# Norm chains of a two-block transformer kernel: row scaling and squares on opposite row halves, and scaled transposes that VectorE writes to SBUF

## What is computed

```
def rms_norm(x, g):
    y = xf * lax.rsqrt(jnp.mean(xf * xf, axis=-1, keepdims=True) + EPS)
    return y * g
...
for l in range(DEPTH_2):
    h = modulate(rms_norm(x, mix_pre_g[l]), sh1, sc1)        # h * (1 + scale) + shift, per column
    p = h @ w_in[l]
    ...
    x = x + g1 * rms_norm(y, mix_post_g[l])
    h2 = modulate(rms_norm(x, ffn_pre_g[l]), sh2, sc2)
    x = x + g2 * rms_norm(sq_relu_mlp(h2, w_ff1[l], w_ff2[l]), ffn_post_g[l])
    # and the same for a second stream, the context, in layer 0
```

## Time and profile before

| | |
|---|---|
| median of three runs | 2186.89 us (2186.88 to 2187.64) |
| the profiled execution's own time | 2187.78 us |
| its span in the profile | 2185.8 us |
| mean granted TensorE clock | 0.988 |
| TensorE, VectorE, ScalarE busy | 95%, 72%, 52% |

### The profile page before, as it was taken

How to read it: one execution, slowest core, us unless ns; L and a number is a source line. 1 busy time by engine, 2 the same in 40 slices (tenths; PEclk the granted TensorE clock), 3 DMA queues, 4 the chain that set the end, 5 groups by cost and what they waited for, 6 DMA issues and landing times.

```text
span 2185.8 us, 31557 instructions
## 1 busy us (share of the span) xinstructions
PE 2086.1 (95%) x12389; PEld 1785.9 (82%) x12389; DVE 1566.2 (72%) x2436; ACT 1129.9 (52%) x1571; POOL 97.2 (4%) x184
## 2 busy tenths in 40 slices
PE   7998989999999999999999999899999999997997
PEld 6776879888877788988887788698978878877996
DVE  5566466577679978655687898765677789976565
ACT  5554444445575446544557544454545674454543
POOL 3100001110000000000000000000000000000000
PEclk9999999999999999999999999999999999999999
DMA  7745467766666645677654444656555444454663
GB/s 253 225 148 188 146 223 249 235 190 203 216 211 193 195 151 168 222 220 227 189 179 130 145 135 142 214 157 191 170 174 184 131 143 126 154 164 145 189 187 106
DMA packets 206371, 394.36 MB, mean 180 GB/s; under 512 B 16471, under 2 KB 19219, under 8 KB 206224
## 3 DMA queue, kind: packets, MB, share of 16 engines
q1 hardware_dynamic: 198624, 381.74, 54.9%
q0 software_dynamic: 7600, 10.61, 1.7%
HBM read 390.98 MB, written 1.30 MB: 179 GB/s over the span
## 4 chain that ended last, share of the span: by engine, by line
PE 83%; DVE 8%; ACT 5%; issue 2%; DMA 2%; DVEq 0%; ACTq 0%; SPq 0%
PE gps L1142 15%; PE gps L1144 14%; PE gps L1143 14%; PE gps L1149 9%; PE gps L1150 9%; PE gps L1151 9%; PE aps L981 2%; PE aps L1104 2%; DVE wlo L1958 2%; PE aps L937 2%; DVE Yc L1801 2%; ACT whi L1464 1%; PE aps L1080 1%; PE aps L1111 1%; PE aps L1067 1%
## 5 line engine op out<-in xcount | busy, mean ns | idle before, releaser
L1958 DVE TENSOR_TENSOR wlo<-raw,whi 128x1024 fp32r<-128x1024 f32 (+1 forms) x648 | 763.3, 1186 | 449.6 <-ACT whi L1464 447.2
L1464 ACT ACTIVATE whi<-raw 128x1024 fp32r<-128x1024 f32 (+1 forms) x648 | 662.6, 1028 | 662.7 <-PE gps L1144 420.2
L1142 PE MATMUL gps<-whi,ohi 128*128 128x512 f32 x1624 | 656.2, 404 | 9.5 <-DVE olo L1829 5.0
L1144 PE MATMUL gps<-whi,olo 128*128 128x512 f32 x1624 | 634.8, 391 | 0.0
L1143 PE MATMUL gps<-wlo,ohi 128*128 128x512 f32 x1624 | 634.4, 391 | 0.0
L1149 PE MATMUL gps<-ohi,whi 128*128 128x256 f32 x1760 | 508.4, 289 | 1.0 <-issue 1.0
L1150 PE MATMUL gps<-olo,whi 128*128 128x256 f32 x1760 | 499.8, 284 | 0.0
L1151 PE MATMUL gps<-ohi,wlo 128*128 128x256 f32 x1760 | 499.5, 284 | 0.0
L1142 PEld LDWEIGHTS gps<-whi,ohi 128*128 128x128 f32 x1624 | 305.8, 188 | 87.2 <-issue 21.0
L1144 PEld LDWEIGHTS gps<-whi,olo 128*128 128x128 f32 x1624 | 305.5, 188 | 65.3
L1149 PEld LDWEIGHTS gps<-ohi,whi 128*128 128x128 f32 x1760 | 339.0, 193 | 20.0 <-issue 19.1
(11 more groups left out here) (284 smaller groups left out, 1544.9 us busy)
## 6 DMA issues: line engine op xcount, KB each, us to landing
raw<-w_in SPq DMA_DIRECT2D x232, 512.0 KB, 3.9
raw<-w_ff SPq DMA_DIRECT2D x192, 512.0 KB, 3.8
raw<-ada_w SPq DMA_DIRECT2D x96, 512.0 KB, 4.4
raw<-w_attn_o SPq DMA_DIRECT2D x24, 512.0 KB, 3.4
raw<-w_gmlp_o SPq DMA_DIRECT2D x24, 512.0 KB, 3.4
raw<-w_conv_o SPq DMA_DIRECT2D x24, 512.0 KB, 3.7
raw<-w_out SPq DMA_DIRECT2D x24, 512.0 KB, 4.7
raw<-w_gate SPq DMA_DIRECT2D x20, 512.0 KB, 4.1
```

The lines of the kernel that those rows point to most:

```text
L1142: mm(om, ah, whi[:, q, i, :], start=first, stop=False)
L1144: t = mm(om, al, whi[:, q, i, :], start=False, stop=last)
L1464: A_(part(whi, jb, q), raw_part(jb, q), ACT.Copy).then_inc(hi_done[q], 1)
L1958: tt(part(wlo, jb, q), raw_part(jb, q), f32(part(whi, jb, q)), ALU.subtract).then_inc(lo_done[q], 1)
```

## The change

1. `T` with a scale: VectorE alone reads the bank, tile by tile (k), applies scale and shift into a slot of 256 columns of `PTb` (four slots), ScalarE copies the slot to `ohi`, VectorE subtracts `ohi` from the slot into `olo`. VectorE's subtraction of tile k stands behind its scaling of tile k + 2. From the third bank on the scaling waits for the subtractions that free its slots.
2. `ycp`: VectorE takes row half 1 first, while ScalarE squares half 0; ScalarE squares half 1 behind it (`y_g`), VectorE takes half 0 behind the first square (`y_sq`).
3. `accy`: the addition is cut in row halves, and ScalarE's first square needs the first half only.
4. `po`: the job j = 0 multiplies and shifts its own sums of squares in advance, so that `po` needs one instruction (L1556) in place of L1552 and L1524.

```diff
@@ ScalarE @@
             def T(p):
-                if p.scale:
-                    wait(act, ("pp_cols", None, 0, 1) if p.scale[0] == "C1" else ("mf_c", None, 0, MODS[p.scale[1:3]] + 1))
                 for b in p.banks:
-                    wait(act, ev("t_pe", p, 4, b + 1))
                     if p.scale:
                         for i in range(2):
                             k = 2 * b + i
-                            t = A_(ohi[:, p.slot, k, :], aps[:, b, i * S:(i + 1) * S], ACT.Identity,
-                                   scale=column(p.scale, k), bias=column(p.shift, k) if p.shift else 0.0)
+                            act.wait_ge(sem["t_y"], 8 * p.of_kind + k + 1)
+                            A_(ohi[:, p.slot, k, :], scaled(k), ACT.Copy).then_inc(sem["t_h"], 1)
...
             def ycp(jb, g):
...
-                sum_squares(jb, tiles(g, 2))
+                sum_squares(jb, tiles(g, 2), lambda m: act.wait_ge(sem["y_g"], jb.n + 1) if m else None)
@@ VectorE @@
             def po(p):
...
-                link(tt(st[:, 5, 0:2], st[:, 5, 0:2], st[:, 5, 2:4], ALU.add))
-                w = rms(5, 2, 1.0 / D)
+                link(stt(st[:, 5, 0:2], st[:, 5, 2:4], CUBIC / D, st[:, 5, 0:2], ALU.mult, ALU.add))
+                w = st[:, 12, :]
+                rsqrt(w[:, 0:2], st[:, 5, 0:2], w[:, 8:10])
...
             def T(p):
...
+                    for b in range(5):
                         for i in range(2):
                             k = 2 * b + i
+                            if b < 4:
+                                if i == 0:
+                                    wait(dve, ev("t_pe", p, 4, b + 1))
+                                    if b > 1:
+                                        wait(dve, ev("t_lo", p, 4, b - 1))
+                                x = aps[:, b, i * S:(i + 1) * S]
+                                if p.shift:
+                                    t = ts(scaled(k), x, column(p.scale, k), column(p.shift, k), ALU.mult, ALU.add)
+                                else:
+                                    t = ts(scaled(k), x, column(p.scale, k), None, ALU.mult)
+                                t.then_inc(sem["t_y"], 1)
+                            if b:
+                                k -= 2
+                                dve.wait_ge(sem["t_h"], 8 * p.of_kind + k + 1)
+                                t = tt(olo[:, p.slot, k, :], scaled(k), f32(ohi[:, p.slot, k, :]), ALU.subtract)
+                                if i:
+                                    t.then_inc(sem["t_lo"], 1)
...
             def ycp(jb, g):
-                gain(jb, tiles(g, 2))
+                dve.wait_ge(used[NQ - 1], jb.i + 1)
+                gain(jb, tiles(g, 2), (1, 0))
...
-                tt(y, y, tiles(g, 2), ALU.add).then_inc(sem["y_add"], 1)
-                dve.wait_ge(sem["y_add"], jb.n + 1)
-                gain(jb, y)
+                for m in range(2):
+                    tt(y[:, m, :], y[:, m, :], tiles(g, 2)[:, m, :], ALU.add).then_inc(sem["y_add"], 1)
+                dve.wait_ge(sem["y_add"], 2 * jb.n + 2)
+                gain(jb, y, (0, 1))
```

More of the change, by code:

```diff
@@ L511, in make_plan @@
             elif k == "T":
+                number(p, "T scaled" if p.scale else "T plain")
+                p.of_kind, p.n = p.n, count["T"] - 1
                 assert 3 not in p.banks or not ad_open
@@ L736, in tiles, with scaled @@
             return ap.rearrange("p (a b) -> p a b", a=a)
+        def scaled(k):
+            return PTb[:, k % 4 * S:(k % 4 + 1) * S]
         def t_step(p, b):
@@ L1429, in ycp @@
                     act.wait_ge(sem["po_x"], 2 * jb.po_before)
-                sum_squares(jb, tiles(g, 2))
+                sum_squares(jb, tiles(g, 2), lambda m: act.wait_ge(sem["y_g"], jb.n + 1) if m else None)
             def accy(jb, g):
-                act.wait_ge(sem["y_add"], jb.n + 1)
                 act.wait_ge(sem["po_x"], 2 * jb.po_before)
-                sum_squares(jb, rows(RB)[:, :, jb.j * NW:(jb.j + 1) * NW])
+                sum_squares(jb, rows(RB)[:, :, jb.j * NW:(jb.j + 1) * NW], lambda m: wait(act, ev("y_add", jb, 2, m + 1)))
             def cgate(jb, g):
@@ new lines, in T @@
+                            if b:
[4 more added lines that the diff above has]
+                                    t.then_inc(sem["t_lo"], 1)
+                    return
+                for b in p.banks:
+                    dve.wait_ge(sem["t_hi"], 4 * p.of_kind + b + 1)
+                    t = stt(olo[:, p.slot, 2 * b:2 * b + 2, :], tiles(bank(b), 2), p.imm, f32(ohi[:, p.slot, 2 * b:2 * b + 2, :]), ALU.mult,
+                            ALU.subtract)
@@ L1891, in acc, with gain @@
                 tt(y, y, tiles(g, 2), ALU.add).then_inc(sem["ac_add"], 1)
-            def gain(jb, src):
+            def gain(jb, src, order):
                 j = slice(jb.j * NW, (jb.j + 1) * NW)
                 dve.wait_ge(sem["gb_in"], 16 * jb.gb)
-                for m in range(2):
-                    dve.wait_ge(sem["y_sq"], 2 * jb.y + m + 1)
+                for m in order:
+                    if order[0] == 0 or m == 0:
+                        dve.wait_ge(sem["y_sq"], 2 * jb.y + m + 1)
                     t = tt(rows(RB)[:, m, j], src[:, m, :], GB[:, j], ALU.mult)
+                    if order[0] == 1 and m == 1:
+                        t.then_inc(sem["y_g"], 1)
                 t.then_inc(sem["y_cp"], 1)
+                if jb.j == 0:
+                    dve.wait_ge(sem["y_sq"], 2 * jb.y + 2)
+                    link(ts(st[:, 5, 0:2], st[:, 5, 0:2], CUBIC / D, EPS * CUBIC, ALU.mult, ALU.add))
                 for p in jb.then:
```

10 lines of the change are left out of this document (6 added, 4 removed).

## The result

| | before | changed |
|---|---|---|
| median of 11 runs each | 2187.67 us | 2193.31 us |
| lowest and highest | 2186.82, 2191.34 | 2190.32, 2198.19 |
| the profiled execution's own time | 2187.78 | 2198.19 |

The ratio is 1.0024 (95% interval 1.0016 to 1.0031, which is 3.5 to 6.8 us): 5.6 us slower, by the medians. The forecast was 2186.3 with a range of 2183.0 to 2190.0. The profiled execution of the changed kernel is the longest of its 11, so its difference to the trace of before, 10.6 us of span, is 5 us more than that of the medians. Where each part of it lies can be read all the same.

A forecast was written before the change was run, and what follows sets the result against it. TensorE, busy 95% of the span, was taken to bound the kernel. Gains 2 x 0.76 + 2 x 0.74 + 0.80 less 0.2, 2.0 and 1.0 gave 0.6 us faster: median 2186.3, range 2183.0 to 2190.0.

The forecast's parts named there:

- t_m: Memory stream's transposes at 42 us: TensorE loses 2.4 us waiting for bank 3, of which 2.0 (1.9 to 2.4) stays.
- post-norms: Two out-projections 0.76 us faster each; `accy` at 1607 us and in the tail 0.74 faster each.
- t_x, t_c, t_f: Scaled transposes at 14, 208 and 292 us: first and last lose 0.1 each at the first bank, the middle one 0.
- `T` at 1620 us: ScalarE held to VectorE's pace delays the key's norm, so TensorE loses 1.0 us (0 to 2.8).
- rival (d): Post-norms: opposite halves do not overlap, the 0.56 twice is lost; 0.5 slower than before, 2187.4 us; 11%.
- Tile price: New `T` on VectorE: scaling and subtraction 0.335 us each per tile, 5.6 for a `T`, by the far ends 7.4.
- Rival (b): Transfers take up the loss at 42 us, which then costs 0.4; 3.7 us faster, 2183.2; 15%.
- 0.52 us at 56.83: TensorE wait behind the ada step, taken up if a weight transfer is not later by all of 2.4 us.
- First bank: Behind the two out-projections: bank ready 0.63 us earlier, worth 0.40 each at half pace, 0.80 together.
- Hidden `T`: Scaled transposes at 491, 849, 879 and 1573 us: cost 0, more if the tile is slower.
- Rival (c): ScalarE held inside `T`: at 0.90 us per tile each `T` is 1.8 longer; 6.2 slower, 2193.1; 14%.

The follow-up runs named there:

- only_tm: The post-norm half of the change plus the new form of the memory stream's scaled transpose at 42 us alone, other ten old: 2189.15 us, ratio 1.0007 to before.
- post_only: The post-norm half of the change alone, all eleven scaled transposes in the old form: 2184.21 us, ratio 0.9987 to the kernel before.
- six: Post-norm half plus new form for the scaled transposes at 491, 849, 879, 1421, 1573 and 1991 us, other five old: 2183.52 us, ratio 0.9982 to before.
- slow_two_old: The changed kernel with the scaled transposes at 42 and 1620 us put back to the old form: 2186.17 us, ratio 0.9991 to before.
- tm_old: The changed kernel with the memory stream's scaled transpose at 42 us put back to the old form: 2188.83 us, ratio 1.0003 to before.
- tm_warm: warm2 with the memory stream's scaled transpose at 42 us alone in the new form, its wait left idle: 2186.84 us, ratio 0.9995 to before.
- tm_warm_fill: tm_warm with 14 thrown-away products on TensorE in the wait at the ada product: 2182.59 us, ratio 0.9979 to before.
- hold4: The kernel before with four extra dependent VectorE instructions ahead of the last bank of the transpose at 42 us: 2191.10 us, ratio 1.0012 to before.
- warm: post_only with 138 thrown-away TensorE products meant for seven idle stretches, eleven of them misplaced: 2185.52 us, ratio 0.9992 to before.
- fill: The changed kernel with 14 thrown-away TensorE products in the wait ahead of the ada product near 48 us: 2192.74 us, ratio 1.0022 to before.
- warm2: warm with its eleven misplaced products moved ahead of the block attention's transposes at 124 us: 2181.47 us (7 runs), ratio 0.9970 to before.

## Why the prediction was wrong

The ladder of ratios, each with an interval of about 0.001 on either side, gives each term a measured size. It starts from before. A step has about 2.8 us on either side: t_m's is clear of nothing (4.4 again in only_tm), the post-norms' as well (2 on either side, as before is the other end), the three between are not, and for them the waits in the traces say more than the times.

| step | ratio | us | predicted |
|---|---|---|---|
| post-norms (post_only) | 0.9987 | -2.8 | -3.0 |
| six hidden or first-bank `T` (six) | 0.9982 | -1.1 | -0.8 |
| t_x, t_c, t_f (slow_two_old) | 0.9991 | +2.0 | +0.2 |
| `T` at 1620 us (tm_old) | 1.0003 | +2.6 | +1.0 |
| t_m (changed kernel) | 1.0024 | +4.6 | +2.0 |

The forecast was 0.6 us faster, and it is 5.3 slower by the ratio. Of the 5.9 between, t_m has 2.6.

1. **Post-norms: right** in mechanism, and in size within the interval. Opposite halves do overlap, so rival (d) falls. In layer 0 the prediction's step from a shorter chain to shorter idle time failed: by the trace the gain went into ScalarE's wait for `w_ff`.
2. **Tile price: mis-sized.** "I take 0.335 for both, since the source, target and size are those of rows 5". The subtraction's starts are 0.33 apart; the scaling's are 0.40 and with a shift 0.45. A tile is 0.73 or 0.79, and a `T` on VectorE 6.3 to 6.8, not 5.6. The row that I took has another form: it multiplies by a constant (0.5), the new one by a column of `C`, and the first takes 0.405 where the second takes 0.48 (248 and 256 columns). The Trainium skill, VectorE: DVE Perf Modes, The TRN2 errata, gives an estimate of 0.39 and 0.33, and the trace agrees with it where there is no shift; the prediction had set it aside.
3. **t_m: the step that failed.** "TensorE loses 2.4 us", of which 2.0 to stay. The wait grew by 3.07, by the tile's price, and the kernel lost 4.6. And the sum held waits only: that a long wait (7.32 us there) is followed by units at half clock stood in the earlier trace rows for 298 us, and I used it there to discount a gain, but never asked whether a wait that I lengthen brings it about where it was not. tm_warm against tm_warm_fill shows it at 2.2 us by the trace; the traces with the 4 us wait put it between 1.5 (hold4, only_tm) and 2.9 (the changed kernel). Rival (b) had t_m at 0.4, and falls by tm_old's 4.6. The 0.52 us at 56.83 that the sum let the transfers take up is in before's trace alone, and in none of the seven others with the old t_m.
4. **1620 us: right mechanism, mis-sized.** ScalarE's copies of the job's result start at 1636.90, 6.1 behind VectorE's first scaling, where I had 5.1. The key's transposes wait 2.46, 1.65 more, not 1.0; half clock behind them (1645 to 1649 us) may be the rest of 2.6. That part wasn't tried by itself.
5. **Missed waits.** t_x 0.78 and t_f 0.71 at the last bank, t_c 1.27: "`t_c` has two units of other work behind it: 0" looked at the units that read the `T` and not at the ada step that waits for bank 3. For t_f I counted the first bank only.
6. **First bank:** 0.27 us sooner in the trace, not 0.63, for the tile's price. The runs don't tell its 0.5 from nothing.
7. **Hidden `T`: right as far as the runs tell.** six is not above post_only.

Rival (c), ScalarE held inside `T`, gave 2193.1, near the measured 2193.3, but with other terms. It asked for 0.84 a tile where 0.79 was enough, had t_m at 4.2 by waiting alone, and losses of 1.8 at hidden places that aren't there. So its sum came out near by accident.

## What to carry to other kernels

When an edit lengthens an engine's share of a hand-over, list every reader of its last output, not of its first: banks that small side jobs share with it as well. Where a wait of TensorE grows to the length at which the rows show half clock behind it (here 3 to 4 us nearly always), add the units behind it at half clock to its price, and where there are such waits already, try work thrown away in them: it was worth 3.7 us here by the ratios (2.7 by the medians), about as much as the post-norm edit. Put it where the engine is idle: eleven products in the wrong place cost all of it in warm. And don't price a new instruction by a neighbour with another operand form where one tile is multiplied by 16.

## What the runs showed of the hardware

- TensorE's granted clock falls to half (1.2 of 2.4 GHz) in or behind an idle stretch, and whether it does at the shorter ones differs from trace to trace, at places where the instructions are the same. Behind 4 us idle at t_m it fell in all four traces that have it (the changed kernel, hold4, only_tm, tm_warm), for 4 to 7 us. Behind the 3.13 us at 124 us it fell in 9 of the 11 traces in which that wait isn't filled, and the stretch from there to the wait at 178 us took 50.3 us in the two without (fill, hold4) and 51.8 to 53.1 in the others (warm aside, where the wait at 178 us is filled). Behind 2.33 us at 750 us it fell in 6 of 15, and cost 1.67 us in the changed kernel's trace (760.36 to 829.83, in before 753.22 to 821.02). Behind 1.95 us at the key's transposes it fell in warm2 and not in warm, tm_warm and tm_warm_fill. Behind 1.66 us (820 us and other places) it fell in none, but at t_c's transposes, which come in two parts with 0.23 us between them, it fell behind 1.59 us in post_only (208 to 213 us) and behind 1.67 us in fill. So the length of the wait alone doesn't tell. This goes with the spread of single executions: in each of the 13 kernels of the experiments, the longer executions tend to have the lower mean clock (correlation -0.66 to -0.92; in fill the shortest, 2186.52 us, has 0.991, the longest, 2195.99, has 0.986), and the spread is 5 to 9 us without the added products, 5.1 in warm, 2.9 in warm2 and 3.6 in tm_warm_fill. That it is the whole cause was not tested.
- So the end of a trace says little of an early edit: hold4's trace has half clock at 50 us and none at 126, before's the reverse, and hold4's span is the shorter by 0.4 us while its median is the longer by 3.7.
- A scaling by one column pointer from PSUM to SBUF, 256 columns in fp32, takes VectorE 0.48 us, with a second pointer for the shift 0.54. By a constant, 248 columns take 0.405.
